# Moving parts of two elementwise passes off VectorE, and a new order of some loads, in a two-layer transformer kernel

## The reference

```python
x = _layer_norm(DEEPNORM_ALPHA * x + g_a * y, ln1_g[l], ln1_b[l])
x = _layer_norm(DEEPNORM_ALPHA * x + g_m * _squared_relu_mlp(x * (1 + sc_m) + sh_m, mlp_w1[l], mlp_w2[l]),
                ln2_g[l], ln2_b[l])
```

## Time and profile before

| | us |
|---|---|
| median of 3 runs | 2968.99 |
| lowest, highest | 2968.83, 2974.59 |
| the profiled execution, its own time | 2971.22 |
| its span, first to last instruction | 2969.4 |
| PE busy in the span | 2793.5 (94%) |
| DVE busy | 1367.4 (46%) |
| ACT busy | 887.6 (30%) |
| POOL busy | 533.5 (18%) |

### The profile page before, as it was taken

The page is one execution under the profiler, slowest core; times in us unless marked ns, Lnnn a source line. Parts: engine busy times, 40 slices in busy tenths (PEclk is TensorE's granted clock), DMA queues, the critical chain, the costliest instruction groups (busy, mean ns, idle before and its releaser), DMA issues. The chain is left out here.

```text
span 2969.4 us, 40552 instructions
## 1 busy us (share of the span) xinstructions
PE 2793.5 (94%) x15615; PEld 2289.2 (77%) x15615; DVE 1367.4 (46%) x2195; ACT 887.6 (30%) x1598; POOL 533.5 (18%) x365
## 2 busy tenths in 40 slices
PE   6999996999999999999969999999697999999998
PEld 3666785788888888888858888888585888888886
DVE  3575554663333333333573565555556333333336
ACT  3244653441211211211132443444342211221222
POOL 0000000341121121111320000000133323323321
PEclk8999998999999999999989999999898999999999
DMA  7584216440010110110331111100455111111112
GB/s 260 189 309 149 75 63 225 123 133 29 29 56 28 39 46 28 42 42 28 85 114 50 36 44 37 36 29 15 129 141 149 57 42 42 57 42 42 57 42 57
DMA packets 202132, 237.42 MB, mean 80 GB/s; under 512 B 15960, under 2 KB 165088, under 8 KB 195872
## 3 DMA queue, kind: packets, MB, share of 16 engines
q1 hardware_dynamic: 201728, 235.74, 24.9%
q10 hardware_dynamic: 288, 0.10, 0.0%
HBM read 203.20 MB, written 36.83 MB: 81 GB/s over the span
## 5 line engine op out<-in xcount | busy, mean ns | idle before, releaser
L2106 DVE TENSOR_TENSOR y<-y,pair 128x1024 f32<-128x1024 f32 x280 | 341.7, 1221 | 337.4 <-PE pair L2275 337.4
L2273 PE MATMUL pair<-m_wbh,m_ath 128*128 128x512 f32 x1080 | 422.1, 391 | 16.8 <-DVE y L2041 16.8
L2275 PE MATMUL pair<-m_wbh,m_atl 128*128 128x512 f32 x1080 | 423.2, 392 | 0.0
L2274 PE MATMUL pair<-m_wbl,m_ath 128*128 128x512 f32 x1080 | 422.2, 391 | 0.0
L1947 ACT ACTIVATE m_rel<-pair 128x512 f32<-128x512 f32 x160 | 88.9, 556 | 1021.0 <-PE pair L2297 1009.9
L2163 DVE TENSOR_TENSOR m_atl<-m_sq,m_ath 128x512 fp32r<-128x512 f32 x150 | 96.4, 644 | 623.1 <-POOL m_sq L2000 623.1
L2000 POOL TENSOR_TENSOR m_sq<-m_rel 128x512 f32<-128x512 f32 x160 | 155.5, 972 | 1124.7 <-ACT m_rel L1947 1124.5
L2297 PE MATMUL pair<-hth,m0n_wal 128*128 128x512 f32 (+1 forms) x768 | 272.2, 354 | 0.0
L2296 PE MATMUL pair<-htl,m0n_wah 128*128 128x512 f32 (+1 forms) x768 | 272.1, 354 | 0.0
L2295 PE MATMUL pair<-hth,m0n_wah 128*128 128x512 f32 (+1 forms) x768 | 271.6, 354 | 0.0
L2273 PEld LDWEIGHTS pair<-m_wbh,m_ath 128*128 128x128 f32 x1080 | 203.4, 188 | 60.7 <-issue 16.3
(11 more groups left out here) (284 smaller groups left out, 5283.7 us busy)
## 6 DMA issues: line engine op xcount, KB each, us to landing
a_ring<-in_w_mod SPq DMA_DIRECT2D x40, 1024.0 KB, 9.4
m_rawb<-in_mlp_w SPq DMA_DIRECT2D x64, 512.0 KB, 4.4
m_rawa<-in_mlp_w SPq DMA_DIRECT2D x60, 512.0 KB, 4.1
x_rows<-r_res SPq DMA_DIRECT2D x26, 512.0 KB, 5.4
r_raw<-cat_cols SPq DMA_DIRECT2D x18, 512.0 KB, 6.4
mod_w<-in_w_mod SPq DMA_DIRECT2D x8, 1024.0 KB, 12.2
r_xin<-in_x SPq DMA_DIRECT2D x16, 512.0 KB, 12.4
gate_pre<-a0g_gout SPq DMA_DIRECT2D x20, 256.0 KB, 2.0
```

What stands on the lines that cost most here:

```text
L2106: dve.tensor_tensor(k.y[:, t, :], k.y[:, t, :], k.pair[t % 2][:, :], ALU.add).then_inc(s_y, 1)
L2273: pe.matmul(o, ath[:, m, ts], bh[:, m, cols], start=m == 0, stop=False)
L2274: pe.matmul(o, ath[:, m, ts], bl[:, m, cols], start=False, stop=False)
L2275: i = pe.matmul(o, atl[:, m, ts], bh[:, m, cols], start=False, stop=m == M - 1)
```

## The change

- The loads at the head are issued in the order gate row 0, `xres` 0, `lng`, `lnb`, the other `xres`, the other gate row; each gate row has its own semaphore. GpSimd waits for `lng` and `lnb` alone, and VectorE waits for the gate row of its tile only.
- `begin_y`: GpSimd does the product of rows and gain (`weigh`), without ALPHA. VectorE scales the shift row by ALPHA once, and then does one instruction for each tile. GpSimd's eight `weigh` stand three ahead of the two L1993 of chunk 0, and 0, 2, 1, 2 after its four `sq`. VectorE's come after each group's two `atl`: four in the first group, three in the second, after `wbl`.
- The last norm: except for the last tile, ScalarE multiplies by the deviation (`deviate`) and GpSimd adds the shift; the last tile's L2140 stays on VectorE and waits for the seven others.

```diff
-            for c in range(3 - XB):
...
-            for t in range(XB):
+            gate_in(0)
+            residual_in(0)
+            for t, name in ((lng, "ln2_g"), (lnb, "ln2_b")) if final else ((lng, "ln1_g"), (lnb, "ln1_b")):
...
+            for t in range(1, XB):
                 residual_in(t)
+            for c in range(1, 3 - XB):
+                gate_in(c)
...
-                        for t in range(EARLY) if g == 0 else range(EARLY, tiles):
+                        some = range(EARLY) if g == 0 else range(EARLY, tiles)
+                        for t in some:
                             spread(t)
+                            if t > some[0]:
+                                deviate(t - 1)
+                        if g == 0:
+                            deviate(EARLY - 1)
+            def deviate(t):
+                act.wait_ge(s_frec, t + 1)
+                act.wait_ge(s_res, t + 1)
+                act.activation(k.y[:, t, :], k.y[:, t, :], ACT.Copy, scale=fstd[:, t % 4, 1:2]).then_inc(s_dev, 1)
...
-            pool.wait_ge(s_row, 48 if final else 64)
+            pool.wait_ge(s_row, 32)
...
+            def weigh(t):
+                if t == 0:
+                    pool.wait_ge(s_begin, 32)
+                pool.wait_ge(s_yx[t], 16)
+                y = by_j(k.y[:, t, :])
+                pool.tensor_tensor(y, y, ln1[0], ALU.mult).then_inc(s_past, 1)
...
+                if starts(c) and final:
+                    for t in range(3):
+                        weigh(t)
...
                         pool.tensor_tensor(sq[:, m % 2, 0:n], r, r, ALU.mult).then_inc(s_sq, 1)
+                        if starts(c) and final:
+                            for t in ((), (3, 4), (5,), (6, 7))[g * M + m]:
+                                weigh(t)
+                    if ends(c) and final:
+                        for t in range(EARLY) if g == 0 else range(EARLY, tiles - 1):
+                            pool.wait_ge(s_lnrow, 32)
+                            pool.wait_ge(s_dev, t + 1)
+                            pool.tensor_tensor(k.y[:, t, :], k.y[:, t, :], lnb2[:, :], ALU.add).then_inc(s_fin, 1)
...
-                        dve.wait_ge(s_yx[t], 16)
                         y = by_j(k.y[:, t, :])
                         if t == 0:
                             dve.wait_ge(s_begin, 32)
-                        dve.scalar_tensor_tensor(out=y, in0=y, scalar=ALPHA, in1=ln1[0], op0=ALU.mult, op1=ALU.mult).then_inc(s_past, 1)
+                            dve.tensor_scalar(ln1[1], ln1[1], ALPHA, None, ALU.mult).then_inc(s_shift, 1)
+                            dve.wait_ge(s_shift, 1)
                         dve.wait_ge(s_past, 2 * tiles + t + 1)
-                        dve.scalar_tensor_tensor(out=y, in0=ln1[1], scalar=ALPHA, in1=y, op0=ALU.mult, op1=ALU.add).then_inc(s_y, 1)
+                        dve.scalar_tensor_tensor(out=y, in0=y, scalar=ALPHA, in1=ln1[1], op0=ALU.mult, op1=ALU.add).then_inc(s_y, 1)
...
-            dve.wait_ge(s_row, 48 if final else 64)
...
+                dve.wait_ge(s_rg[cond(t)], 16)
                 dve.wait_ge(s_yps, t + 1)
...
                 dve.reciprocal(fstd[:, t % 4, 1:2], fstd[:, t % 4, 0:1]).then_inc(s_frec, 1)
+                if t < tiles - 1:
+                    return
                 dve.wait_ge(s_frec, t + 1)
                 dve.wait_ge(s_res, t + 1)
+                dve.wait_ge(s_fin, t)
...
-                        if final and starts(c):
-                            begin_y(1, tiles)
                     for m in range(M):
...
                         dve.tensor_tensor(atl[:, m, a:a + n], sq[:, m % 2, 0:n], f32(ath[:, m, a:a + n]), ALU.subtract).then_inc(s_atl, 1)
+                    if final and starts(c):
+                        begin_y(*((1, 5), (5, tiles))[g])
```

More of the change, by code:

```diff
@@ L1685, in stage_block @@
     rsem = lambda n: k.sem(f"{rtag}_{n}")
-    s_row, s_xr, s_past, s_begin = rsem("rows"), [rsem(f"x{i}") for i in range(XB)], rsem("past"), rsem("begin")
+    s_row, s_xr, s_past, s_begin, s_shift = rsem("rows"), [rsem(f"x{i}") for i in range(XB)], rsem("past"), rsem("begin"), rsem("shift")
     s_raw = [rsem(f"raw{i}") for i in range(2)]
@@ L1689, in stage_block @@
     s_dve, s_std, s_g, s_b, s_tr, s_mod, s_hh, s_hl, s_half = [rsem(x) for x in ("dve", "std", "g", "b", "tr", "mod", "hh", "hl", "half")]
+    s_rg = [rsem(f"rgate{c}") for c in range(2)]
     s_lnr, s_lnt, s_fold = rsem("lnr"), rsem("lnt"), rsem("fold")
@@ L1724, in stage_block @@
     s_grow, s_lnrow, s_bg, s_fstd, s_fin = sem("grow"), sem("lnrow"), sem("bg"), sem("fstd"), sem("fin")
+    s_dev = sem("dev")
     s_yx, s_out, s_centre, s_frec = [sem(f"yx{t}") for t in range(XT)], [sem("out0"), sem("out1")], sem("centre"), sem("frec")
@@ L1786, in _, with gate_in @@
             sp.wait_ge(s_wlow, KT)
+            def gate_in(c):
+                sp.dma_start(rgate[:, c, :].rearrange("p (j q) -> p j q", q=P),
+                             bass.AP(tensor=k.gate_dram.tensor, offset=(layer * 2 * 2 * KT + c) * P, ap=[[0, P], [2 * P, KT], [1, P]])).then_inc(s_rg[c], 16)
+            gate_in(0)
+            residual_in(0)
             for t, name in ((lng, "ln2_g"), (lnb, "ln2_b")) if final else ((lng, "ln1_g"), (lnb, "ln1_b")):
                 sp.dma_start(t[:, :], bass.AP(tensor=io[name].tensor, offset=0, ap=[[0, P], [1, D]])).then_inc(s_row, 16)
-            for c in range(3 - XB):
-                sp.dma_start(rgate[:, c, :].rearrange("p (j q) -> p j q", q=P),
-                             bass.AP(tensor=k.gate_dram.tensor, offset=(layer * 2 * 2 * KT + c) * P, ap=[[0, P], [2 * P, KT], [1, P]])).then_inc(s_row, 16)
-            for t in range(XB):
+            for t in range(1, XB):
                 residual_in(t)
+            for c in range(1, 3 - XB):
+                gate_in(c)
             for t in range(tiles):
```

## The result

The changed kernel is slower: its median is 2981.14 us over 11 runs (2976.10 to 2984.31), that of the kernel before, run beside it 11 times in all, 2970.92 (2968.83 to 2974.59; the three runs shown ahead are among these). The ratio is 1.0036, with a 95% interval of 1.0027 to 1.0044, so some 10 us. The profiled execution took 2980.06 us with a span of 2978.3, 8.9 longer than that of before. TensorE does the same number of matmuls (15615), was busy for 2788.4 us (before 2793.5), and so was idle 14.0 us longer.

The account below looks back on a forecast made before the run. The prediction took TensorE, busy for 94% of the span, to bound the kernel except where it waits. Its terms, -6.9 - 0.3 + 14.9 + 0.8 = +8.5 us on 2968.99, gave 2977.5 us, range 2961 to 2985.

Parts of the forecast that it names:

- Head of layer 0: Layer 0's first loads: TensorE's 4.65 us wait and 2.3 us of slow clock behind it go, -6.9 us.
- `cat_in(2)` costs nothing: Head of layer 0: work behind tile 0 is a row of equal tiles, so nothing takes the -6.9 us back.
- Rival C: Head of layer 0 gives nothing: `cat_in(2)` or `xres` 0 lands late, TensorE's wait stays elsewhere; +15.4 us, 2984.4 us, chance 0.07.
- Head of layer 1: GpSimd's first product waits for `lnb`, fourth load as `xres` 0 was; -0.3 us, between -1.5 and +1.
- Beginning of the sums: Layer 1's first sums: VectorE and GpSimd instructions take turns, delaying TensorE's second product; +14.9 us, bounds -6.5 and +19.
- tile 0 at the slow clock: Beginning of layer 1's sums: TensorE's tile 0 takes 5.3 us, with `begin_y` 7 done within it.
- The end: Last norm: GpSimd's shift sums and L2135 take turns and the last L2140 waits; +0.8 us, bounds -1.9 and +3.
- The hold: The end: last L2140 waits for tile 6's shift sum, starting at 2964.5 instead of 2963.95; +0.5 us.
- the store term: The end: the last store follows tile 6's by 1.3 us and shares the transfer engines; +0.3 us, an estimate.
- The bound of -1.9: The end without turns: the shift sums end 2.4 us sooner, giving -1.9 us.
- Rival A: Beginning of sums: turns, but GpSimd's chunk-1 work not between; 8.8 us less, whole -0.3, 2968.7 us, chance 0.20.
- Rival B: VectorE and GpSimd overlap: beginning -6.5, end -1.9, with heads -15.6 us, 2953.4 us; chance 0.15.

Follow-up runs that it names:

- `head_cat`: Kernel before with the new load order at the heads and, in layer 0, `cat_in(2)` third in order; median 2966.53 us, ratio 0.9985 to the kernel before.
- `head_pool_late`: Kernel before with the new head loads and GpSimd's chunk-1 work held until `k.y` is begun, old `begin_y` kept; median 2960.24 us, ratio 0.9969.
- the PSUM operand: Changed kernel with `begin_y`'s VectorE instruction reading its second operand from PSUM, first norm's shift left out (timing only); median 2967.17 us, ratio 0.9985 to before.
- rival A's test: Changed kernel with GpSimd starting chunk 1's work only when all eight tiles of `k.y` are begun; median 2973.58 us, ratio 1.0007 to the kernel before.

## Why the prediction was right

The forecast was +8.5 us, measured were +8.9 between the profiles and +10.2 between the medians. The direction, the place and the mechanism were right. That the two totals are so close is in part luck: the four changed stretches give +11.3 us between the profiles, 2.8 more than the forecast, and the stretches that are the same in both kernels took back 2.5. One term was off by 2.5 us, two by 1.0.

- **Head of layer 0, -6.9 forecast, -4.4 measured.** The wait of 4.65 us is gone, as said: with the head's first matmul as origin, tile 0's transposes came at 24.43 us before, and at 19.63 both with `head_cat` and with `head_pool_late`, 4.8 earlier. In the changed kernel's profile they came at 20.97, as the granted clock in the first 5 us was 0.69 there (16 matmuls) and 1.00 before (22). That is 1.3 us of this one execution; over all profiles the stretch from the head's first matmul to the last transposes is 131.8 to 132.9 us with the old order (four) and 126.1 to 127.7 with the changed one (six), 5.1 less on the mean. From these transposes to the last ones the forecast was -2.3, measured were -0.95 (107.38 to 106.43): the step that failed is that `cat_in(2)` costs nothing. Rival C named this load, but counted it at the whole wait. It costs 1.07 us, since it lands when GpSimd's first gain product starts, and VectorE's split of it has two SBUF inputs and took a turn behind that product, 2.36 us instead of 1.23. At 1.23 it would have ended at 519.3, before TensorE was ready (520.55 - 1.07 = 519.5), so in this profile the turn is the whole wait. `head_cat` shows the 1.4 us that come back.
- **Head of layer 1, -0.3 forecast, +0.7 measured**, inside its bounds. In this pair of profiles `lnb` as fourth landed 0.7 us later than `xres` as fourth had, which is within what executions of one order differ by.
- **Beginning of the sums, +14.9 forecast, +13.9 measured.** The turn-taking of the earlier trace rows carried it. The wait for `htl` was forecast near 8 us (8.9), that for `begin_y` at 26 (26.0), TensorE's start of `second` 16.1 us later (16.3 from the last transposes: 54.80 against 38.49). VectorE's instruction took up to 3.3 us where a GpSimd one stood beside it, and GpSimd's chunk-1 work stood before the last. The step that was off is "tile 0 at the slow clock" for 5.3 us: the clock rose in the third microsecond (last section), and the stretch from TensorE's start to the second sum was 2.4 us shorter than before, where I had 1.2.
- **The end, +0.8 forecast, +1.1 measured.** A pair costs 3.3 us (13.24 for four), VectorE's last instruction starts when the last shift sum is done. The hold, forecast at +0.5, came to 1.05, and the store term (+0.3) to 0.1. The bound of -1.9 leaves out the store term; with it, it is -1.6.
- **Rival A** fell: chunk 1's work was between, and the test that moves it away gives about the 8.8 us it was priced at: 8.6 by the ratios, 7.4 in the profiles' stretch. **Rival B** fell with the 3.3 us; its condition, `begin_y` not held by `weigh`, was made true by the PSUM operand (1209 ns). Even so its price of -6.5 for the beginning didn't come: the stretch was 0.8 us longer than before, with `wbl` and `atl` still held. Without any turns at all nothing was run.
- **The base.** The three runs shown of before were on the low side: 2968.99 against 2970.92 over 11. The forecast was put on the first, so 1.9 of the 3.6 us between 2977.5 and 2981.14 are from there.

## What to carry to other kernels

Before moving elementwise work from VectorE to GpSimd, look in the trace for stretches where both work on two SBUF operands: there a moved instruction saved nothing on VectorE in this kernel, since each of its remaining ones waited for one of GpSimd's (3.3 us a pair for 128x1024, 1.22 alone). An operand in PSUM, where banks are free and ScalarE can fill them once, took VectorE's instruction out of it; the others that still read two operands from SBUF stayed held. Where PSUM has no room, GpSimd's work that nobody waits for yet is best put behind VectorE's. When a burst of loads is put in a new order, follow each load to its first user, the one behind the burst too.

## What the runs showed that was not expected

**TensorE's clock at the same place differs between executions.** The granted clock in the first 5 us of layer 0's head, with the same instructions before it in each kernel. Columns: stretch, length, busy time and instructions of PE, PEld, DVE, ACT, POOL, clock, share of DMA, GB/s. Kernel before, then the kernel with the end alone:

```profile
498.80:503.80 5.00, 4.99 (x22) 4.15 (x23) 5.00 (x5) 5.00 (x6) 0.00 (x0) 1.00 0.00 0
```

```profile
497.00:502.00 5.00, 5.00 (x12) 3.94 (x13) 5.00 (x5) 5.00 (x6) 0.00 (x0) 0.50 0.00 0
```

0.50 is the level of 1.2 GHz and 1.00 that of 2.4. TensorE did 22 matmuls in one and 12 in the other, behind the same filling matmuls. The Trainium skill ("TensorE: Matmul & The Clock Gate", What's actually happening) says that the number of slow matmuls at a kernel's start varies between runs of the same kernel. The rows here show the like in the middle of a kernel, between executions of two kernels that are the same up to this place.

**The like is seen behind a stall.** The first 4 us behind the wait for `begin_y`, kernel after (26 us of wait) and the kernel of rival A's test (17 us):

```profile
2283.50:2285.50 2.00, 2.00 (x5) 1.61 (x6) 0.87 (x1) 0.00 (x0) 0.00 (x0) 0.50 0.00 0
2285.50:2287.50 2.00, 2.00 (x9) 1.60 (x8) 0.00 (x0) 0.00 (x0) 0.00 (x0) 0.79 0.00 0
```

```profile
2281.00:2283.00 2.00, 2.00 (x6) 1.57 (x5) 0.00 (x0) 0.00 (x0) 2.00 (x2) 0.50 0.00 0
2283.00:2285.00 2.00, 2.00 (x6) 1.54 (x5) 0.43 (x1) 0.00 (x0) 2.00 (x2) 0.54 0.35 90
```

The clock rose sooner behind the longer stall, but with `head_pool_late` it rose as soon (0.50, then 0.78) behind one of 11.3 us, so the length of the stall alone does not decide. What does is open. A microsecond or two of any single profile is of this kind; it is why a term of this size should be read from differences inside one execution, and its sign from the runs.
